# Positive parts of the indexer added from PSUM, and the last chunk of the first mixer's projection behind the second logits of its attention

## The reference

```python
def even_mixer(h, w_in, w_out, cmp_pe, cmp_w, rel_tab):
    qa, kva, ga, qb, kb, vb, iq, ik, iw = split_cols(h @ w_in, EV_SIZES)
    o_a = nsa_mixer(qa, kva, ga, rel_tab[:, :A_HEADS], cmp_pe, cmp_w)
    o_b = dsa_mixer(qb, kb, vb, iq, ik, iw, rel_tab[:, A_HEADS:A_HEADS + B_HEADS])
    return jnp.concatenate([o_a, o_b], axis=-1) @ w_out
```

```python
        idx_logit = jax.nn.relu(jnp.einsum('bthd,bsd->bths', iqb, ik).astype(jnp.float32))
        idx_score = jnp.einsum('bth,bths->bts', iwb.astype(jnp.float32), idx_logit)
        idx_score = jnp.where(key_pos[None, :] <= t[:, None], idx_score, NEG_INF)
        _, sel = lax.top_k(idx_score, k_top)
```

## Time and profile before

| | us |
|---|---|
| median of 3 runs | 2196.02 |
| lowest, highest | 2195.72, 2197.43 |
| the profiled execution | 2195.4 |
| its span on the core | 2193.6 |

### The profile page before, as it was taken

One profiled execution on the slowest core, in us unless ns is written; L12 is line 12 of the kernel. 1 busy time (PEld: TensorE's weight loads), 2 busy tenths in 40 slices (PEclk: granted clock), 3 DMA queues, 4 the chain that ended last, 5 costly groups with the idle time before them and its releaser, 6 DMA issues.

```text
span 2193.6 us, 32260 instructions
## 1 busy us (share of the span) xinstructions
PE 2158.2 (98%) x11554; PEld 1819.9 (83%) x11554; DVE 1094.8 (50%) x2183; ACT 532.3 (24%) x1234; POOL 1376.8 (63%) x878
## 2 busy tenths in 40 slices
PE   8999999999999999999999999999999999999997
PEld 6888889788888988888898888888777988888886
DVE  5544302699845665551066554016466458555312
ACT  4111002417824611110040000014355344111000
POOL 6666666675267576666677666656424847666664
PEclk9999999999999999999999999999999999999998
DMA  6433333320133133333323332323212412333331
GB/s 238 157 96 96 90 97 101 122 68 20 59 109 103 59 106 97 97 96 93 100 79 107 98 97 89 97 89 105 63 44 88 125 58 87 96 96 96 95 98 48
DMA packets 62414, 206.11 MB, mean 94 GB/s; under 512 B 6831, under 2 KB 9263, under 8 KB 61924
## 3 DMA queue, kind: packets, MB, share of 16 engines
q1 hardware_dynamic: 55168, 187.79, 28.0%
q10 hardware_dynamic: 7140, 16.90, 2.2%
HBM read 201.98 MB, written 8.70 MB: 96 GB/s over the span
## 4 chain that ended last, share of the span: by engine, by line
PE 89%; DVE 6%; POOL 2%; ACT 2%; issue 1%; DMA 0%; ACTq 0%; POOLq 0%; DVEq 0%
PE bank L930 27%; PE bank L931 27%; PE bank L932 27%; PE bank L1315 1%; PE bank L1286 1%; DVE top L2454 1%; PE bank L1254 1%; PE bank L1171 1%; PE bank L1203 1%; POOL w_lo L712 1%; POOL sq_sum L751 1%; PE bank L958 1%; PE bank L1186 1%; PE bank L1257 0%; DVE sq_sum L2457 0%
## 5 line engine op out<-in xcount | busy, mean ns | idle before, releaser
L712 POOL TENSOR_TENSOR w_lo<-w_raw,w_hi 128x1024 fp32r<-128x1024 f32 (+1 forms) x354 | 855.5, 2417 | 29.5
L930 PE MATMUL bank<-h_hi,w_hi 128*128 128x512 f32 (+1 forms) x2136 | 798.1, 374 | 1.8 <-DVE h_lo L2147 0.9
L931 PE MATMUL bank<-h_lo,w_hi 128*128 128x512 f32 (+1 forms) x2136 | 791.0, 370 | 0.0
L932 PE MATMUL bank<-h_hi,w_lo 128*128 128x512 f32 (+1 forms) x2136 | 790.9, 370 | 0.0
L710 POOL TENSOR_SCALAR w_hi<-w_raw 128x1024 fp32r<-128x1024 f32 (+1 forms) x354 | 373.9, 1056 | 632.8 <-PE bank L932 399.0
L930 PEld LDWEIGHTS bank<-h_hi,w_hi 128*128 128x128 f32 x2136 | 402.8, 189 | 75.9 <-issue 4.2
L932 PEld LDWEIGHTS bank<-h_hi,w_lo 128*128 128x128 f32 x2136 | 402.6, 188 | 69.4
L931 PEld LDWEIGHTS bank<-h_lo,w_hi 128*128 128x128 f32 x2136 | 403.0, 189 | 66.5
L930 PE MATMUL bank<-act_hi,w_hi 128*128 128x512 f32 (+1 forms) x792 | 290.0, 366 | 0.0
L931 PE MATMUL bank<-act_lo,w_hi 128*128 128x512 f32 (+1 forms) x792 | 289.4, 365 | 0.0
L932 PE MATMUL bank<-act_hi,w_lo 128*128 128x512 f32 (+1 forms) x792 | 289.4, 365 | 0.0
(11 more groups left out here) (301 smaller groups left out, 2148.5 us busy)
## 6 DMA issues: line engine op xcount, KB each, us to landing
w_raw<-in_w_up SPq DMA_DIRECT2D x176, 512.0 KB, 3.5
w_raw<-in_w_down SPq DMA_DIRECT2D x64, 448.0 KB, 3.2
w_raw<-in_w_down SPq DMA_DIRECT2D x32, 512.0 KB, 3.5
w_raw<-in_w_ev_in SPq DMA_DIRECT2D x19, 512.0 KB, 3.5
w_raw<-in_w_xkv SPq DMA_DIRECT2D x16, 512.0 KB, 3.5
w_raw<-in_w_od_in SPq DMA_DIRECT2D x16, 512.0 KB, 3.5
bias_line_rows<-bias_lines ACTq DMA_DIRECT2D x1, 6400.0 KB
ev_strip<-bias_line_rows ACTq DMA_DIRECT2D x16, 256.0 KB, 3.0
```

Of the source, the lines that this page charges most:

```text
L712: pool.tensor_tensor(w_lo[j][:, 0:cols], raw[j][:, 0:cols], w_hi[j][:, 0:cols].bitcast(F32), ALU.subtract).then_inc(split_done, 1)
L930: pe.matmul(out, w_hi[j][:, w], hi, start=first, stop=False)
L931: pe.matmul(out, w_hi[j][:, w], lo, start=False, stop=False)
L932: return pe.matmul(out, w_lo[j][:, w], hi, start=False, stop=last)
```

## The change

Three things change, all in layer 0's mixer.

1. ScalarE takes the positive part in place: it reads the bank and writes the same bank. The four SBUF buffers are gone, and with them ScalarE's waits for `idx_added`. VectorE's additions read the bank. TensorE waits for `idx_added` (four more additions) ahead of a group, where it waited for `relu_done`.
2. Where half a chunk (4 tiles) stood between two groups of index products, now 5 tiles stand behind each of the first four groups and 6 behind the last two (`IDX_AT`; `pieces` counts tiles across chunks). Chunks 6 to 9 are made so; before, 6 to 8 were.
3. Chunk 18 goes to bank 4 (`B_O[1]`), and its products are issued behind the logits of the second group. VectorE copies it at the end of its step 1. The first logits' third bank, 2, no longer waits for it: it waits for chunk 14, whose bank it takes.

```diff
--- before.py
+++ after.py
@@ -57,9 +57,9 @@
 POOL_LAST = 5
 TAIL_POOL, TAIL_DVE = (1, 3, 5), (0, 2, 4, 6, 7)
 N_LOGIT, N_PROB, N_PROBT = 3, 5, 3
-IDX_RING = 4
 
 SCALE_AT, TURN_AT, OUT_AT = 3, 4, 6
+IDX_AT = (0, 5, 10, 15, 20, 26, 32)
 Q_TURN, Q_OUT, Q_LEAVE = 2, 3, 4
 QB_LOGIT, QB_TURN = (0, 1, 2), (5, 6, 7)
 N_SETS, SET, Q_RING = 3, 2 * (NT + 1) * P, 8
@@ -221,8 +221,6 @@
     cmp_pe = m.put("cmp_pe", [P, 2, CMP_LEN], F32)
     top8 = m.put("top8", [P, NT - 1, 8], F32)
     at = m.at
-    n = Region(at + 6144)
-    relu = [n.put(f"relu{j}", [P, T], F32) for j in range(IDX_RING)]
     score = [ev[:, VG, :], sq[0][:], sq_sum[:]]
     ev_y = Region(at).put("ev_y", [P, KC, T], F32)
 
@@ -299,6 +297,8 @@
             return B_SPARE
         if kind == "od_in" and c >= OD_FIRST:
             return (c + 1) % 2
+        if kind == "ev_in" and c == EV_IN - 1:
+            return B_O[1]
         if kind == "down" and c == KC - 1 and half == 1:
             c -= 1
         return (CHUNK[name] + c) % R
@@ -1239,7 +1239,7 @@
                     masked = []
                     for b, jobs in enumerate(g["banks"]):
                         if phase == 0 and s == 0:
-                            pe.wait_ge(chunk_out, CHUNK["ev_in"] + EV_IN - 2 + b)
+                            pe.wait_ge(chunk_out, CHUNK["ev_in"] + (EV_IN - 2, EV_IN - 1, EV_IN - 4)[b])
                         if phase == 3 and s == 0:
                             k = (QB_LOGIT[b] - CHUNK["ukv"]) % R
                             pe.wait_ge(q_nope, 4 + 4 + k + 1)
@@ -1268,8 +1268,6 @@
 
                 def turn(s):
                     g = groups[s]
-                    if phase == 0 and s == 0:
-                        pe.wait_ge(rows_done, V_ROWS["ev_v"] + 2 + 7)
                     for b, jobs in enumerate(g["banks"]):
                         if g["copied0"][b]:
                             pe.wait_ge(bank_copied[b], g["copied0"][b])
@@ -1291,6 +1289,8 @@
                     to = bank[B_O[g["f"] % 2]]
                     if g["opens"] and g["f"] >= 2:
                         pe.wait_ge(lo_done, SPLIT[OUT_KEY[phase]] + g["f"] - 1)
+                    if phase == 0 and g["opens"] and g["f"] == 1:
+                        pe.wait_ge(chunk_out, CHUNK["ev_in"] + EV_IN)
                     if phase == 3 and g["opens"] and g["f"] == 1:
                         pe.wait_ge(sub_normed, D_HEADS)
                     if g["kind"] == "cmp":
@@ -1371,37 +1371,38 @@
                 pre_norm(s, "ev_in")
                 c0 = CHUNK["ev_in"]
 
-                def half_chunk(c, part):
-
-                    u, b = UNIT["ev_in"] + c, c0 + c
-                    if part == 0:
-                        pe.wait_ge(split_done, u + 1)
-                        pe.wait_ge(chunk_out, b - R + 1)
-                    for k in range(4 * part, 4 * part + 4):
-                        mm = product(b % R, u % R, k, h_hi[:, k, :], h_lo[:, k, :], k == 0, k == KC - 1)
-                    if part:
-                        mm.then_inc(unit_done, 1)
+                def pieces(first, n):
+
+                    for at in range(first, first + n):
+                        c, k = divmod(at, KC)
+                        u, b = UNIT["ev_in"] + c, c0 + c
+                        if k == 0:
+                            pe.wait_ge(split_done, u + 1)
+                            pe.wait_ge(chunk_out, b - R + 1)
+                        mm = product(bank_of("ev_in", c), u % R, k, h_hi[:, k, :], h_lo[:, k, :], k == 0, k == KC - 1)
+                        if k == KC - 1:
+                            mm.then_inc(unit_done, 1)
 
                 def index_logits(n):
 
                     i, first = 1 + n // 2, 4 * (n % 2)
                     if n:
-                        pe.wait_ge(relu_done, 4 * n)
+                        pe.wait_ge(idx_added, 4 * n)
                     for j in range(4):
                         e = slice(IDX_DH * j, IDX_DH * j + IDX_DH)
                         pe.matmul(bank[4 + j][:, 0:P * (i + 1)], ev[e, IQ + first // 4, P * i:P * i + P],
                                   ev[e, IK, 0:P * (i + 1)], start=True, stop=True).then_inc(idx_done, 1)
 
-                half_chunk(R + 1, 0)
+                pieces(KC * (R + 1), 4)
                 pe.wait_ge(chunk_out, c0 + R + 1)
                 turn_rows("vg", 0, ev[:, VG, :], NT)
-                half_chunk(R + 1, 1)
+                pieces(KC * (R + 1) + 4, 4)
                 pe.wait_ge(rows_done, V_ROWS["vg"] + 1)
                 for n in range(6):
                     index_logits(n)
-                    half_chunk(R + 2 + n // 2, n % 2)
-                chunks("ev_in", EV_IN - 1, R + 5, h_hi, h_lo)
-                pe.wait_ge(relu_done, (NT - 1) * IDX_HEADS)
+                    pieces(KC * (R + 2) + IDX_AT[n], IDX_AT[n + 1] - IDX_AT[n])
+                chunks("ev_in", EV_IN - 1, R + 6, h_hi, h_lo)
+                pe.wait_ge(idx_added, (NT - 1) * IDX_HEADS)
                 pe.wait_ge(rows_done, V_ROWS["vg"] + 1)
                 for k, src in enumerate((VS, VW)):
                     pe.wait_ge(chunk_out, c0 + src + 1)
@@ -1413,12 +1414,17 @@
                         mm = pe.matmul(bank[4 + kv][0:DH, 0:2 * N_CMP], cmp_w[:, kv, l, :], cmp_x[:, kv, l, :, :],
                                        start=l == 0, stop=l == CMP_LEN // 2 - 1)
                     mm.then_inc(cmp_done, 1)
-                chunks("ev_in", EV_IN, EV_IN - 1, h_hi, h_lo)
                 pe.wait_ge(rows_done, V_ROWS["ev_v"] + 5)
                 for g in range(2):
                     mm = pe.transpose(bank[4][0:N_CMP, P + DH * g:P + DH * g + DH], vcT[:, g, :], ident[0:DH, 0:DH])
                 mm.then_inc(cmp_done, 1)
-                quad_attention(0)
+
+                def last_chunk():
+
+                    pe.wait_ge(rows_done, V_ROWS["ev_v"] + 2 + 7)
+                    pieces(KC * (EV_IN - 1), KC)
+
+                quad_attention(0, {1: last_chunk})
                 out_projection("ev_out", s, 0, KC, range(KC))
 
             def cross(s, n):
@@ -1879,10 +1885,8 @@
                 for k in range((NT - 1) * IDX_HEADS):
                     i = 1 + k // IDX_HEADS
                     act.wait_ge(idx_done, k + 1)
-                    if k >= IDX_RING:
-                        act.wait_ge(idx_added, k - IDX_RING + 1)
-                    act.activation(relu[k % IDX_RING][:, 0:P * (i + 1)], bank[4 + k % 4][:, 0:P * (i + 1)],
-                                   ACT.Relu).then_inc(relu_done, 1)
+                    out = bank[4 + k % 4][:, 0:P * (i + 1)]
+                    act.activation(out, out, ACT.Relu).then_inc(relu_done, 1)
                 c0 = CHUNK["ev_in"]
 
                 def k_high(n):
@@ -1892,7 +1896,6 @@
 
                 act.wait_ge(chunk_out, c0 + KS + 1)
                 k_high(0)
-                act.wait_ge(idx_added, (NT - 1) * IDX_HEADS)
                 k_high(1)
                 act.wait_ge(chunk_out, c0 + KW + 1)
                 k_high(2)
@@ -2438,7 +2441,7 @@
                     dve.wait_ge(relu_done, k + 1)
                     if h:
                         dve.wait_ge(idx_added, k)
-                    dve.scalar_tensor_tensor(sc, relu[k % IDX_RING][:, 0:w], ev_v[:, 2, i, 88 + h:89 + h],
+                    dve.scalar_tensor_tensor(sc, bank[4 + k % 4][:, 0:w], ev_v[:, 2, i, 88 + h:89 + h],
                                              sc if h else ev_causal[:, off:off + w], ALU.mult,
                                              ALU.add).then_inc(idx_added, 1)
                 dve.wait_ge(idx_added, (NT - 1) * IDX_HEADS)
@@ -2462,11 +2465,11 @@
                     dve.wait_ge(dve_done, n_small[0] - NT + 2 + i)
                     dve.tensor_scalar(taken_mask[:, i, 0:P * (i + 2)], sc, TAKEN / 2, NEG, ALU.is_gt,
                                       ALU.mult).then_inc(mask_done, 1)
-                for _ in range(EV_IN):
+                while out[0] < EV_IN - 1:
                     leave_next()
 
-                dve.wait_ge(chunk_out, CHUNK["ev_in"] + EV_IN)
-                quad_attention(0)
+                dve.wait_ge(chunk_out, CHUNK["ev_in"] + EV_IN - 1)
+                quad_attention(0, {1: leave_next})
                 memory(0)
                 output_chunks(s + 1, "ev_out", ev_y, lambda c: c + 1, 0, R)
                 rsqrt(("mem", 0), MT, D)
```

## The result

| | before | after |
|---|---|---|
| median, us | 2196.07 (22 runs, 2195.13 to 2198.30) | 2200.6 (22 runs, 2198.73 to 2201.95) |
| span of the profiled execution, us | 2193.6 | 2198.8 |
| mean granted clock | 0.996 | 0.994 |

The ratio is 1.002, with a 95% interval of 1.0014 to 1.0026. So the change costs 4.5 us (3.1 to 5.7), which is just about the 4.4 us that I took as the bound between no change and slower. The forecast was 2198.5, with a range of 2194.3 to 2201.4.

A forecast was written before the change was run, and what follows sets the result against it. TensorE was taken to bound the kernel, except VectorE between 415 and 499 us. Fifth logits +1.1 us by the order, +2.5 with half clock, gave 2196.0 + 2.5 = 2198.5 us, range 2194.3 to 2201.4.

The forecast's parts named there:

- Parts 1 and 2: Index stage: PSUM additions lose 8.3 us of stalls; the new handshake fits, TensorE's group distances leave VectorE 0.8 to 0.9.
- The rival of the long handshake: Index stage: positive part plus additions outlast their room of about 0.2 us per group, so groups wait; chance 0.14.
- Part 3: Attention start: chunk 18 behind the second logits puts 5.5 us on the path; fifth logits 1.1 us later.
- Part 4: Attention start: half clock returns after TensorE's idle time, making +1.1 to +3.7 us in all; +2.5 taken.
- The bound of 0.9: First attention logits: a half-clock stretch covering them lengthens them by up to 0.9 us.
- The chunk's bound of 1.7: Chunk 18's products behind the second logits: a half-clock stretch covering them costs up to 1.7 us.
- the end that holds: Attention start: by the skill, products behind each long wait start at the low rate, giving the upper end, +3.7 us.
- the 1.7 us of half clock in the kernel before: Before the fifth logits: 3.4 us at 1.2 GHz, counted as a loss of 1.7 us absent from the new sum.
- The rival "VectorE keeps the 8.3 us": Index stage: group distances don't bind, so the fifth logits come 4.5 us earlier; chance 0.08, shared with any unseen gain.

The follow-up runs named there:

- e5: e4 with the groups of index products four tiles apart instead of five and six; 2197.2 us, ratio 1.0004.
- e4: Changed kernel, but chunk 18 made in bank 6 ahead of the first logits and copied in VectorE's step 0; 2196.61 us, ratio 1.0002 to before.
- e3: Changed kernel plus 24 unused products into bank 7 ahead of the first logits, where TensorE waits; 2198.82 us, ratio 1.0011 to before.
- e6: Kernel before, with only chunk 18 moved to bank 6, still ahead of the first logits, and copied later; 2196.32 us, ratio 1.0001.
- e7: Kernel before, with only the index groups' distance changed to five and six tiles, positive parts staying in SBUF; 2197.75 us, ratio 1.0004.
- e9: Changed kernel with index groups four tiles apart, chunk 18 staying behind the second logits; 2198.7 us, ratio 1.001 to before.
- e1: Changed kernel with chunk 18 back in its old bank and place, so the index-stage change alone; 2195.65 us, ratio 0.9999 to before.
- e10: e4 with index groups 5, 4, 5, 5 and 6 tiles apart; 2195.53 us, ratio 0.9998 to before.
- e2: Kernel before, with only chunk 18 moved to bank 4 behind the second logits, index stage as it was; 2200.86 us, ratio 1.0023.
- e8: e3 with 12 unused covering products instead of 24; 2201.09 us, ratio 1.002 to before.

## Why the prediction was right, and where not

**Parts 1 and 2 were right in kind and size.** Additions from PSUM at 0.48, 0.62 and 0.75: measured 0.483, 0.618, 0.751, without a long one. Group distances within 0.05 us. VectorE keeps 0.95 us where 0.8 to 0.9 was forecast. The stalls themselves were 8.9 us rather than 8.3: that is what the seven long additions took beyond the undisturbed ones, and the two copies among them cost 0.4 us each and not 0.6. Since TensorE's distances set the pace, nothing hung on it. The rival of the long handshake fell: no group waits, and its room can be read from e5, where the last group's chain is 5.15 us (436.19 - 431.04), the number of the forecast. One thing was not in it: I named VectorE as the engine of this stretch and gave no bound for TensorE's waits there. In the kernel before the wait of 1.04 us is harmless, since TensorE still comes to the second bank 0.58 us ahead of VectorE. In e5 the waits are 2.55 us, 1.5 more, which is beyond this room, and the second bank comes 1.0 us later than before and 1.9 later than in e4.

**Part 3 was right at full clock.** Second bank 0.9 earlier: 1.05. Chunk 5.5: e3 has 5.47. Compressed logits to fifth 5.9: 5.91. The fifth logits 1.1 later than before: e3, which has this order at full clock, has 97.98 against 97.06, so 0.9.

**Part 4 was right in kind and too small.** The low stretch came back and reached into the chunk's products, as taken. I put the loss in the logits at up to 0.9 us and in the chunk at up to 1.7, and took 1.4 for both. By e3 it is 1.73 and 0.86, 2.6 in sum. The bound of 0.9 is the term that failed: I thought the logits were paced by the drains and that a slower TensorE would hide behind them. At 1.2 GHz TensorE becomes the slower of the two. The step from one 128x512 product to the next is 0.43 us there (499.01, 499.44, 499.86), and 2.70 us become 4.43. The stretch, moreover, was not 3.4 us long but 10.2, of which 6.2 lay behind the last wait. The chunk's bound of 1.7 erred the other way, so that the two bounds together, 2.6, are what was measured; that is luck. The sentence drawn from the Trainium skill (TensorE: Matmul & The Clock Gate, "HAM oscillation") set +3.7 as the end that holds; the trace agrees in that all products right behind the wait run at the half rate. By it the fifth logits would be 3.7 us late; they are 3.3 (100.40 against 97.06).

**A term of 0.8 us was missing.** From the fifth logits to the output projection before takes 96.92 us, and after 97.72. It is no cost of the change. Eight other kernels of the table have 97.68 to 97.76 as well, and only those with a low stretch just ahead of the fifth logits (before, e5) have 96.9. I had taken the 1.7 us of half clock in the kernel before as fully on the path, since TensorE was busy there. But a kernel without it (e6) gains only 0.5: 1.4 us from the fourth to the fifth logits, less the 0.15 of its own hole and 0.8 given back within ten microseconds behind the fifth logits. From these to the product at 519.66 the kernel before takes 8.89 us, e6 to the same product (519.15) 9.71. Before, then e6:

```profile
519.66 0.55 PE L1286 MATMUL bank<-ident,ev_sets 128*128 128x128 f32 x3 [0.29 <-ACT probT_sets L1814]
```
```profile
511.63 1.09 PE L1319 MATMUL bank<-probT_sets,ev_v_rows 128*64 128x128 f32 x16 [0.16 <-ACT probT_sets L1824]
...
519.15 0.55 PE L1290 MATMUL bank<-ident,ev_sets 128*128 128x128 f32 x3 [0.44 <-ACT probT_sets L1824]
```

The holes in which TensorE waits for ScalarE are 0.31 us wider in e6 (0.16 + 0.44 against 0.29). The rest of the 0.8 lies between turns and outputs that start further apart, with no hole in the trace, and what holds them is not shown. The 1.7 should have been about 0.6.

Forecast against trace, from the first index group to the output projection: +1.1 for the order and +1.4 for the clock gave +2.5. Measured is +0.9, +2.4 (the 3.34 at the fifth logits less the 0.9) and +0.8, thus +4.1. That is beyond the upper bound of the sum, +3.7. The measured time lies in the range only because I had added 1.7 us for a low stretch that comes or goes further on, and no such stretch made the 0.8.

**The rival "VectorE keeps the 8.3 us"** fell, as the trace of before said it would: TensorE's products set the distances. e5 shows that a closer spacing would not have brought them either.

Left open: what decides whether a low stretch falls at 505, 750 or 1610 in a kernel whose holes are small. The one near 750 is in the traces of e4, e7 and e9, behind holes of 0.24 and 0.47 us that all the kernels have there. With stretches of 1.7 us each that come and go, the kernels e1, e4, e6 and e10 and the kernel before can't be put in order by time. That e10 beats the kernel before is likely by its trace up to the output projection (193.40 against 193.98) and not shown by its median.

## What to carry to other kernels

Work of the busiest engine that lies under a wait is free there. Move it out, and it costs its full length wherever it lands, unless the wait goes as well: here 5.5 us moved out of a wait onto the path, and the holes that it filled gave back only 2.0, so read the width of the holes first. A new wait of several microseconds on TensorE also costs what follows it: here the half clock went on for 5.2 (e2) to 6.7 us (e9) of products behind the last wait. A cover that left a wait of 2.12 us right ahead of the logits (e8) bought nothing, one that left 0.54 (e3) bought 2.4 us; what lies between was not tried. And where two engines arrive nearly together, price an edit against both, as the same spacing lost 1.9 us at the second bank in e5 and gained 0.95 in e9.

## What the runs showed of the hardware

- Low clock at the start of this attention came in stretches of 3.4, 6.8 and 10.2 us. It began within waits of TensorE or behind holes, and in the changed kernel it lasted 6.2 us beyond the last wait, with TensorE busy (498.42 to 504.6). All twelve traces have a further stretch of 3.4 us that begins at 1621.6 to 1628.2 us, so it makes no difference between them.
- A scalar_tensor_tensor with one operand in PSUM is as fast as with both in SBUF (751 ns at 128x512), and was never held up beside GpSimd's splits (0.754 us at most). The one with both in SBUF took up to 2.70 us. The splits ran faster too: 2.39 us in the mean against 2.50 in that stretch. The Trainium skill (SBUF — State Buffer, "Who interferes with whom") states that a VectorE instruction with two SBUF inputs contends with a GpSimd instruction that reads SBUF and that one with a single SBUF input, outside the modes that use both ports, does not; the traces of before, after and e7 agree.
- ScalarE's positive part from PSUM to PSUM takes 0.376 us at 128x256 and 0.589 at 128x512 in the mean (0.388 and 0.599 into SBUF), so the place of its result matters by 0.01 us.
- Two profiled executions of the same code can stand 1 us apart before the first change in the code, by the arrival of the first transfers. Counting from a common instruction takes that out.
